# A four-tile encoder layer: the loops of all engines written out at build time

## The reference

```
h = rmsnorm(x);  z = h @ w_in                       # 1024 x 5120 columns: u v q f i og gates
a = gelu(u) * (block-causal w @ layernorm(gelu(v)) + b)          # gMLP, 4 heads, 128-blocks
b = rmsnorm(HGRN2(silu(q), forget(f), i)) * silu(og)             # 4 heads, 128x128 state
x = x + (sig(gate_a) * (a @ w_br_gm) + sig(gate_b) * (b @ w_br_hg)) @ w_out
h = rmsnorm(x);  z = causal_conv3(h @ w_up) + conv_b             # 2 x 2816 columns
x = x + (silu(z[:2816]) * z[2816:]) @ w_down;  return rmsnorm(x)
```

## Time and profile before

| | us |
|---|---|
| median of 3 runs | 3103.34 (3100.92 to 3103.46) |
| span of the profiled execution, first to last instruction | 3099.1 |
| PE busy | 2924.7 (94%) |
| DVE busy | 2245.1 (72%) |
| POOL busy | 1232.8 (40%) |
| ACT busy | 908.1 (29%) |

### The profile page before, as it was taken

One profiled execution on the slowest core, in us unless ns is written; L12 is line 12 of the kernel. 1 busy time (PEld: TensorE's weight loads), 2 busy tenths in 40 slices (PEclk: granted clock), 3 DMA queues, 4 the chain that ended last, 5 costly groups with the idle time before them and its releaser, 6 DMA issues.

```text
span 3099.1 us, 43292 instructions
## 1 busy us (share of the span) xinstructions
PE 2924.7 (94%) x13492; PEld 2398.1 (77%) x13492; DVE 2245.1 (72%) x3126; ACT 908.1 (29%) x1099; POOL 1232.8 (40%) x507
## 2 busy tenths in 40 slices
PE   7999998899999999889999999888999999988898
PEld 6888877778888887777888888777788888776776
DVE  4885789976388569996547857999654874799964
ACT  4332322223333232222333323222233332322222
POOL 3333434344423344444443344344443324433443
PEclk9999999999999999999999999999999999999998
DMA  4213222233322322223231232222333213222232
GB/s 164 75 68 108 95 83 86 81 115 102 123 68 74 108 95 81 85 85 115 102 123 61 71 119 89 87 81 81 122 103 116 68 64 125 89 83 86 82 122 102
DMA packets 75835, 293.78 MB, mean 95 GB/s; under 512 B 8416, under 2 KB 8672, under 8 KB 73312
## 3 DMA queue, kind: packets, MB, share of 16 engines
q1 hardware_dynamic: 75744, 292.63, 27.4%
HBM read 282.11 MB, written 10.49 MB: 94 GB/s over the span
## 4 chain that ended last, share of the span: by engine, by line
PE 51%; DVE 34%; issue 11%; DVEq 2%; ACT 1%; DMA 0%; ACTq 0%; SPq 0%
PE bank L791 13%; PE bank L792 13%; PE bank L795 13%; DVE conv L750 8%; DVE g_f L755 6%; DVE conv L746 3%; PE bank L851 3%; DVE z L741 2%; DVE g_lo L759 2%; DVE kp L619 2%; PE bank L838 2%; PE bank L840 2%; PE bank L839 2%; DVE total L620 2%; DVE g_hi L757 2%
## 5 line engine op out<-in xcount | busy, mean ns | idle before, releaser
L344 POOL TENSOR_TENSOR w_lo<-raw,w_hi 128x1024 fp32r<-128x1024 f32 x498 | 1227.7, 2465 | 1841.8 <-ACT w_hi L354 1841.5
L791 PE MATMUL bank<-h_hi,w_hi 128*128 128x512 f32 x2400 | 958.3, 399 | 113.3 <-DVE z L741 113.3
L354 ACT ACTIVATE w_hi<-raw 128x1024 fp32r<-128x1024 f32 x496 | 526.0, 1060 | 1741.3 <-PE bank L795 1574.6
L792 PE MATMUL bank<-h_lo,w_hi 128*128 128x512 f32 x2400 | 941.2, 392 | 0.0
L791 PEld LDWEIGHTS bank<-h_hi,w_hi 128*128 128x128 f32 x2400 | 454.0, 189 | 243.3 <-ACT w_hi L354 141.0
L795 PE MATMUL bank<-h_hi,w_lo 128*128 128x512 f32 x2400 | 593.3, 389 | 0.0
L792 PEld LDWEIGHTS bank<-h_lo,w_hi 128*128 128x128 f32 x2400 | 454.2, 189 | 94.5 <-issue 1.9
L795 PEld LDWEIGHTS bank<-h_hi,w_lo 128*128 128x128 f32 x2400 | 450.5, 188 | 93.6
L750 DVE SCALAR_TENSOR_TENSOR conv<-z,params,conv 128x512 f32<-128x512 f32 x352 | 327.0, 929 | 53.6 <-DVE conv L750 26.8
L791 PE MATMUL bank<-g_hi,w_hi 128*128 128x512 f32 x704 | 276.8, 393 | 12.4 <-DVE g_lo L759 6.7
L792 PE MATMUL bank<-g_lo,w_hi 128*128 128x512 f32 x704 | 274.1, 389 | 0.0
(11 more groups left out here) (188 smaller groups left out, 3488.9 us busy)
## 6 DMA issues: line engine op xcount, KB each, us to landing
raw<-w_units SPq DMA_DIRECT2D x498, 512.0 KB, 3.3
x_in<-x_t SPq DMA_DIRECT2D x10, 1024.0 KB, 7.1
out<-res SPq DMA_DIRECT2D x4, 2048.0 KB, 8.0
res<-x_t SPq DMA_DIRECT2D x4, 2048.0 KB, 8.3
out<-res SPq DMA_DIRECT2D x4, 512.0 KB, 3.2
masks<-masks_in SPq DMA_DIRECT2D x1, 1152.0 KB, 11.8
gm_w<-gm_wt SPq DMA_DIRECT2D x1, 256.0 KB, 8.3
lnb_row<-ln_b SPq DMA_DIRECT2D x1, 256.0 KB, 8.8
```

Source lines behind the costliest of these rows:

```text
L344: po.tensor_tensor(w_lo[j][:, :, :], raw[j][:, :, :], w_hi[j][:, :, :].bitcast(F32), ALU.subtract).then_inc(lo_made, 1)
L354: act.activation(w_hi[slot][:, :, :], raw[slot][:, :, :], ACT.Copy).then_inc(hi_made, 1)
L791: pe.matmul(dst, w_hi[slot][:, off + k, :], rhs_hi(k), start=first and k == 0, stop=False)
L792: pe.matmul(dst, w_hi[slot][:, off + k, :], rhs_lo(k), start=False, stop=False)
```

## The change

Every loop on the engines becomes a loop of the program that builds the kernel, so that its body stands in the instruction stream once for each iteration, with numbers in place of the loop's variables. There are sixteen places, all alike (and 18 blank lines go at the head of the file, so that the lines after it are numbered 18 lower):

```diff
-            with sp.Fori(0, (last - first) // 2) as i:
+            for i in range(0, (last - first) // 2):
...
-        with po.Fori(0, (NT * UNITS + 2) // 2) as i:
+        for i in range(0, (NT * UNITS + 2) // 2):
...
-        with act.Fori(0, NT) as t:
+        for t in range(0, NT):
...
-            with act.Fori(1, KF) as f:
+            for f in range(1, KF):
...
-            with dve.Fori(0, NH) as h:
+            for h in range(0, NH):
...
-            with dve.Fori(0, KF) as f:
+            for f in range(0, KF):
...
-        with pe.Fori(0, NT) as t:
+        for t in range(0, NT):
...
-            with pe.Fori(1, KF) as f:
+            for f in range(1, KF):
```

More of the change, by code:

```diff
@@ L311, in _ @@
         sp.dma_start(masks[:, :], masks_in).then_inc(masks_here, 16)
-        with sp.Fori(0, NT) as t:
+        for t in range(0, NT):
             stream(t, 0, 6)
@@ L408, in _ @@
             act.wait_ge(out_sent, t * 16 + 16)
-            with act.Fori(0, NH) as h:
+            for h in range(0, NH):
                 it = t * NH + h
@@ L442, in _ @@
                     weights_hi(t, U_MIX + 4 * p + 2 + j)
-            with act.Fori(0, KD // 2) as p:
+            for p in range(0, KD // 2):
                 it = t * (KD // 2) + p
@@ L570, in final_out @@
                                          op1=ALU.mult).then_inc(*fin_dve.did(f"o{c}"))
-        with dve.Fori(0, NT) as t:
+        for t in range(0, NT):
             dve.memset(scores[:, :], 0.0).then_inc(*zero_dve.did("scores"))
@@ L704, in _ @@
             dve.memset(sum_r[:, :], 0.0).then_inc(*zero_dve.did("sum_out"))
-            with dve.Fori(0, KD // 2) as p:
+            for p in range(0, KD // 2):
                 dve.wait_ge(*zero_dve.at("sum_out", t))
@@ L876, in _ @@
                 for_tokens(t, n, bank[4:8], False)
-            with pe.Fori(0, NH) as h:
+            for h in range(0, NH):
                 it = t * NH + h
@@ L935, in _ @@
                 branches(j, 0)
-            with pe.Fori(1, KD // 2) as p:
+            for p in range(1, KD // 2):
                 gates(p * 4, t * B_TILE + p + B_MIX)
```

## The result

The changed kernel takes 3028.59 us (median of 4 runs, 3027.8 to 3028.64), the kernel before, on the same chip, 3102.59 us (4 runs, 3100.92 to 3103.46). The ratio is 0.9763, 95% interval 0.975 to 0.9777: 74.0 us less. The forecast was 3029 us. The profiled span went from 3099.1 to 3026.8 us, 72.3 less. In what follows a line of the kernel after is 18 lower than the same line before.

What follows compares the result with a forecast made beforehand. The prediction took PE to bound five stages and DVE the up stage: 84 x 0.80 = 67 us plus 6.5 elsewhere, 74 us; span 3025, median 4.2 us above it, 3029 us; range 3002 to 3074.

Steps and rivals of the forecast that it cites:

- The gaps: DVE in up: gaps before L750, L757 and L759 fall to L616's 0.034 us, 0.47 + 0.18 us a step.
- Halo and first tap, second half: DVE in up: L744 and L746 overlap their predecessors as in the first half, saving 0.29 us a step.
- What is lost again: DVE in up: first-half L741 and L755, with two waits each, come out worse, costing 0.14 us a step.
- The locks: POOL's two locks a step in up keep their present cost; bounds: the step saves 1.1 or 0.35 us.
- the sum: DVE's step in up: every gap counts, as in the prediction, 0.80 us a step.
- The rival that the locks absorb it: Up stage: DVE arrives early at each locked operation and waits there, 0.35 us saved a step, 3070 us; chance 0.13.
- PE as the bound: Rival, up stage: the step falls to PE's floor of 11.2 us, 2967 us; chance 0.04.
- Late fetches: Rival, DVE in up and heads: late instruction blocks stop the engine 3.76 us each, 3142 us; chance 0.08.
- The small terms: Savings outside the up steps: PE's tile loop, End of up, Heads and norms, together 6.5 us.
- Heads: PE's wait for L620 in the heads: 0.1 us saved in each of 16 heads, 1.5 us.
- End of up: PE's wait for the last L759 of up: the last step shorter by 0.8 us each time, 3 us.
- PE's tile loop: PE's branch back, taken three times, of which 0.32 us shows each: 1 us saved.

Runs made afterwards that it cites:

- fixed_taps: Kernel before with all loops kept, only the scalar of L750's two taps read from a fixed column: 3078.8 us, ratio 0.9925.
- dve_up_loop_only: Kernel before with only DVE's loop over the up steps written out, its tile loop kept: 3044.32 us, ratio 0.9814.
- own_wait_first: Changed kernel with the wait for DVE's own last result named first before L723 and L737: 3017.8 us, ratio 0.9726.
- first_half_gaps: Changed kernel with a second, long satisfied wait before the two L732 taps of the first half only: 3031.86 us, ratio 0.9774.
- all_but_dve: Kernel before with the loops of SP, POOL, ACT and PE written out, DVE's kept: 3099.01 us, ratio 0.9987.
- dve_only: Kernel before with only DVE's four loops written out: 3038.94 us, ratio 0.9797.
- own_wait_last: Changed kernel with a second, long satisfied wait named first before each L732 tap, four times a step: 3050.69 us, ratio 0.9833.
- half_lock: Changed kernel with POOL computing only half of each w_lo but the first two: 2917.5 us, ratio 0.9403.
- dve_makes_w_lo: own_wait_first with DVE instead of POOL making w_lo for 41 of 44 up units in each tile: 2940.75 us, ratio 0.9481.

## Why the prediction was right, and where its bookkeeping was not

**The whole.** 3029 against 3028.59 us, and the interval 11.92 against 11.94. The likeliest case is the one that came. That it came within 0.5 us is luck. The forecast put the median 4.2 us above the span, as it was before, but every run's time lies 1.8 us above its own span, and the other 2.4 us were that profiled run's distance from the median. The span was forecast as 3025 and is 3026.8.

**The gaps.** Right. Before L732, L739 and L741 they are 0.034 to 0.035 us. The cause that was given, the sequencer's address computation with the wait sitting on it, is shown for the taps: fixed_taps takes away only the address, dve_up_loop_only keeps thresholds that vary with the tile, and both have the short gap.

**Halo and first tap, second half.** L724 starts at 1303.44 and L728 at 1303.64, 0.20 apart; before it was 1279.69 to 1280.13, 0.44. 0.24 us, forecast 0.29.

**What is lost again.** Right in kind, a little dearer. L723 starts 0.14 us behind L741 of the step before, and L737 0.11 behind the tap; 0.18 us for both, forecast 0.14. It was not inevitable: own_wait_first gets it back.

**The locks.** Two statements of the forecast went wrong. One is that POOL's second operation "stays at 7.9 us" in DVE's step: it came at 7.67 (below). The other is "I let both locks cost what they cost now". As a ledger it nearly holds for the step shown: 0.47 from the taps' gaps, 0.24 from the halo, 0.19 from L739 and L741, less 0.18, is 0.72, and the two locks, with the overlap of the rows behind the first, then cost 0.14 less; together 0.86 of 12.80 - 11.93 = 0.87. But fixed_taps took one term of it alone and got 0.28 for 0.47, and first_half_gaps put two small terms back and paid almost nothing. The terms do not add up one by one, because most of them stand ahead of a lock.

The account that fits the single steps is the deadline. The rows of before that it needs, DVE's end of the step shown in the earlier trace rows:

```profile
1273.90 0.69 DVE L741 TENSOR_TENSOR z<-bank,rms_inv 128x512 f32<-128x512 f32 x1
...
1282.52 2.77 DVE L755 TENSOR_TENSOR g_f<-silu,conv 128x512 f32<-128x512 f32 x1
1285.43 0.43 DVE L757 TENSOR_SCALAR g_hi<-g_f 128x512 f32 x1
...
1286.70 0.69 DVE L741 TENSOR_TENSOR z<-bank,rms_inv 128x512 f32<-128x512 f32 x1
```

POOL asks at 1281.81, 7.91 us after L741; its row ends 2.93 later at 1284.74; L755 ends at 1285.29, 0.55 behind it; the next L741 starts 1.41 behind that. The same four numbers for one usual step of each kernel, in us, read from its rows. (In before, steps of 12.67 and 12.81 us alternate; the one shown above is of the longer kind, the table has the shorter.)

```
                  POOL asks  its row  held op ends  behind it   step
before                 7.93     2.78          0.54       1.42  12.67   L755 held
fixed_taps             7.93     2.52          0.55       1.43  12.43   L755
all_but_dve            7.66     2.39          0.55       2.15  12.75   last tap
dve_up_loop_only       7.91     2.40          0.55       1.22  12.08   L755
dve_only               7.91     2.92          0.28       0.86  11.97   L757
after                  7.67     2.39          0.56       1.31  11.93   L737
own_wait_last          7.70     2.53          0.55       1.32  12.10
own_wait_first         7.70     2.39          0.55       1.22  11.86
first_half_gaps        7.66     2.42          0.55       1.32  11.95
```

Read along a row this is bookkeeping, for four stretches of one step make up the step. Down a column it says where time can come from. The first column has two values only: 7.9 with the other engines' loops, 7.7 without. No DVE gap that was added or taken away moved it. The second is 2.39 plus POOL's wait for the DVE operation under way, which an earlier DVE can only bring to zero. The last two depend on which operation is held. So the shorter usual step's 12.67 - 11.93 = 0.74 us are: 0.26 from POOL asking earlier, 0.39 from POOL not waiting (0.54 in the longer kind), and 0.1 from the gaps behind the lock (0.19 saved before L739 and L741, 0.10 lost to L723's double wait). The means differ by 0.78, for before's mean also has the longer kind in it, 16 of 84 steps of 13.0 us, where the last tap is held and L755 stands behind the lock, and some shorter ones.

It also gives the 6 us that neither half of the change has. all_but_dve has POOL asking early, but DVE is then only at the start of its last tap, the lock falls on that, and L755's 0.7 us moves behind it:

```profile
1306.46 2.96 DVE L750 SCALAR_TENSOR_TENSOR conv<-z,params,conv 128x512 f32<-128x512 f32 x1 [0.15 <-DVE conv L750]
```

dve_only has DVE early but POOL late. Why T fell by 0.26 can be read from the traces, link by link. Half is PE: its first matmul starts 0.05 us behind the end of L723 (1298.68 to 1298.73), before it was 0.18 (1274.59 to 1274.77, rows 3). The other half is ACT, whose copy starts 0.04 us behind the end of PE's unit where it was 0.17 (medians of 80 steps; in the steps shown PE's units end at 1280.50 and 1304.48). PE's unit itself, ACT's 1.06 us and POOL's start 0.08 us behind ACT are the same in both kernels. ACT's sequencer instruction (count, ns min/median/max) and its copy before, then the copy after:

```profile
L353 ACTq FUSED_REGOPS  x120: 37/86/96, 30.2 to 2949.6; - x120
```

```profile
1280.66 1.06 ACT L354 ACTIVATE w_hi<-raw 128x1024 fp32r<-128x1024 f32 x1 [0.83 <-PE bank L795]
```

```profile
1304.52 1.07 ACT L336 ACTIVATE w_hi<-raw 128x1024 fp32r<-128x1024 f32 x1 [0.93 <-PE bank L777]
```

Here no address is computed, for ACT's slots are fixed in both kernels. ACT names two waits, for PE's unit and then for the load (L353), and the second one's threshold is computed by an instruction of 86 ns, which carries the first wait. PE has the same at L789, 85 ns. So a computation between a wait and the operation costs its time, 0.13 us here, be it of an address or of a threshold; the taps' thresholds cost nothing because they are computed while the operation before still runs.

The deadline is not the whole either. Of the three kernels that were to tell it from the sum, only first_half_gaps came out at its number; the medians of own_wait_last and own_wait_first are the sum's. It forecast the usual step of those two within 0.04 us, but not their means, which depend on the steps in which a lock catches another operation. What decides how many steps are of that kind is open, and with it which theory would give the time of a further kernel.

The Trainium skill, SBUF — State Buffer, section "SBUF: two separate sides", has the lock going to whoever starts first, for its whole instruction; the trace agrees, in both directions: POOL's row is 2.39 us when it finds the ports free and 2.93 when a DVE operation is under way. The forecast took from it that a gap saved just before a locked operation is worth nothing, and then did not apply it to the sum. One DVE operation stands outside: the bank read. In 60 of before's steps POOL begins while L741 still has 0.1 to 0.5 us to run, and POOL's row is 2.36 to 2.40 us long all the same.

**The rival that the locks absorb it** was put at 0.13 with 3070 us. Its mechanism is at work, as fixed_taps and first_half_gaps show, but its price assumed that DVE was already waiting at the lock. It was POOL that waited for DVE, 0.39 or 0.54 us of the usual steps, and that was there to be gained.

**PE as the bound.** The floor was taken as 11.2 us; half_lock and dve_makes_w_lo show 10.88. Taking the recorded wait off the step left in what the stop costs beside it: in before PE's units start 7.25 and 5.57 us apart, and 5.44 where PE never stops. PE still waits about 0.7 us a step in the changed kernel, 57.7 us in all, forecast 55 to 60.

**Late fetches.** Did not happen: twice the instruction packets on q8, no idle time of DVE in up without a releaser, and on PE's weight loads, which run beside the matmuls, the short places named above, 11.4 us in all at these two lines where before had 13.5. The Trainium skill, Runtime: NRT & Kernel Launch, section "Instruction fetch mechanics", has forward code fetched ahead of its use; the trace agrees.

**The small terms.** Heads were to give 1.5 us, and PE's wait there stayed at 11.9: nothing. End of up was to give 3 us and PE's tile loop 1: PE's wait for the last g_lo fell from 6.7 to 2.4 us, and down with the end of up and the tail lost 6.1 us over the four tiles, 1.5 in the second where "within 1 us" was forecast. The start of the kernel took some 2 us more, which no term foresaw. The sums still agree: counted as the forecast counts, in intervals, the steps of up brought 84 x 0.78 = 66 us of the 72.3 (67 forecast) and all the rest 6.7 (6.5 forecast). For the rest that is luck, since its terms did not come out one by one.

## What to carry to other kernels

Where two engines exclude each other, find which one waits for the other at each lock: in the usual steps here, time saved ahead of the lock counted only as far as the lock's owner was waiting, and time saved behind it counted in full. The mean over all steps did not follow this rule in two kernels of three. A gap of 0.15 us in front of a dependent operation, beside a sequencer instruction that computes an address or a second threshold, went away when these were numbers, at the price of a longer program, for which no row here shows a cost. And when an engine is slowed by locks on a neighbour's work, price that work on the engine itself: here 1.22 us a unit instead of 2.1.

## What the runs showed of the hardware

- Of several waits in front of one DVE operation, the order written decides the gap: own last result named last, 0.10 to 0.14 us; named first, 0.03 to 0.04. Exchanging them in two places was worth 11 us.
- A sequencer's address computation with a wait on it costs 0.152 - 0.035 = 0.12 us in front of each operation. A threshold computed ahead costs nothing that shows (dve_up_loop_only); one computed behind another wait costs 0.13 us (ACT's copy 0.17 against 0.04 us behind PE, PE's first matmul 0.18 against 0.05 behind DVE).
- A POOL operation that waits gets the ports at the next boundary between two DVE operations: in before's step it asked at 1281.81, during a tap, and L755, started at 1282.52, was the one held. It does so too where DVE's next operation starts 0.03 us behind (in four steps of own_wait_first POOL asks during L737, and L739 is held).
- The DVE operation held ends 0.55 us behind POOL's end if it is a 128x512 tap or product, 0.28 to 0.29 if it is L757. In no step of up, in before, after or the seven kernels of the table besides, was the bank read (L741, L723) held: its longest row is 0.69 us. Nor does POOL wait for it.
- 128x1024 fp32 subtraction: 2.39 us on POOL, 1.22 on DVE.
